# 384 dense columns, 40 tiles turned ahead, and loads and norm in other places: a hybrid attention, mLSTM and expert step

## What is computed

```
x = x + merge(attention(xn), mlstm(xn))           # xn = rmsnorm(x) * g1, one input projection
q = (xn @ wq).reshape(nb, 8, 2, 64)               # xn = rmsnorm(x) * g2
s = einsum('nhpd,hpkd->nhpk', q, sub_keys)        # 128 keys on each side
sv, si = top_k(s, 16)
cand = sv[:, :, 0, :, None] + sv[:, :, 1, None, :]
fv, fi = top_k(cand, 16)                          # 16 of 16384 experts for each of 8 heads
eidx = experts of fi;  g = softmax(fv)
act = gelu(einsum('nhkd,nd->nhk', peer_u[eidx], xn))
x = x + einsum('nhk,nhkd->nd', g * act, peer_v[eidx])
```

## Time and profile before

| | us |
|---|---|
| runs | 2080.23, 2080.6, 2068.4; median 2080.23 |
| profiled execution | 2077.23, span 2075.5, mean granted clock 0.961 |
| PE, PEld busy in the span | 1922.2 (93%), 1819.3 (88%) |
| DVE, ACT, POOL busy | 1344.6 (65%), 892.0 (43%), 963.4 (46%) |
| moved by DMA | 478.80 MB, mean 231 GB/s |

### The profile page before, as it was taken

The page is one execution under the profiler, slowest core; times in us unless marked ns, Lnnn a source line. Parts: engine busy times, 40 slices in busy tenths (PEclk is TensorE's granted clock), DMA queues, the critical chain, the costliest instruction groups (busy, mean ns, idle before and its releaser), DMA issues. The chain is left out here.

```text
span 2075.5 us, 32520 instructions
## 1 busy us (share of the span) xinstructions
PE 1922.2 (93%) x11569; PEld 1819.3 (88%) x11569; DVE 1344.6 (65%) x2582; ACT 892.0 (43%) x1936; POOL 963.4 (46%) x840
## 2 busy tenths in 40 slices
PE   7999959998896999999999999998799999999997
PEld 6978748886895999898998899997799999999996
DVE  2134435555513299798999766774387877777775
ACT  4031113234304245677777777774233333333333
POOL 4433303332221257789999999995022222222210
PEclk9999979998997999999999999999899999999999
DMA  7611187786407145698999899999599999999982
GB/s 170 123 52 47 36 221 232 234 242 220 149 21 152 35 148 181 215 283 264 276 290 281 257 285 297 291 301 289 186 318 355 328 348 338 346 346 331 356 300 82
DMA packets 325245, 478.80 MB, mean 231 GB/s; under 512 B 37436, under 2 KB 249916, under 8 KB 321756
## 3 DMA queue, kind: packets, MB, share of 16 engines
q1 hardware_dynamic: 288220, 342.49, 53.9%
q0 software_dynamic: 36864, 134.23, 20.2%
HBM read 391.52 MB, written 83.96 MB: 229 GB/s over the span
## 5 line engine op out<-in xcount | busy, mean ns | idle before, releaser
L1413 PE MATMUL ps<-x_high,uT_high 128*128 128x416 f32 x1024 | 373.8, 365 | 20.6 <-DVE uT_low L1400 17.9
L1670 POOL TENSOR_SCALAR area<-iota_row,chosen 128x128 f32<-128x128 f32 x416 | 387.1, 944 | 3.2
L2013 PE MATMUL ps<-hid_high,v_high 128*128 128x416 f32 x1024 | 360.1, 352 | 12.7 <-DVE hid_low L1986 12.7
L1413 PE MATMUL ps<-x_high,uT_low 128*128 128x416 f32 x1024 | 364.5, 356 | 0.0
L1413 PE MATMUL ps<-x_low,uT_high 128*128 128x416 f32 x1024 | 361.9, 353 | 0.0
L2013 PE MATMUL ps<-hid_low,v_high 128*128 128x416 f32 x1024 | 359.9, 351 | 0.0
L2013 PE MATMUL ps<-hid_high,v_low 128*128 128x416 f32 x1024 | 359.7, 351 | 0.0
L1281 POOL DMA_INDIRECT gathered_rows<-in_peer_v_dram,gathered_index x128 | 134.9, 1054 | 430.5 <-DVE gathered_acc L1318 350.4
L1957 ACT CAST v_high<-area 128x1024 fp32r<-128x1024 f32 x128 | 134.3, 1049 | 390.8 <-PE ps L2013 386.9
L1984 DVE TENSOR_TENSOR v_low<-area,v_high 128x1024 fp32r<-128x1024 f32 x128 | 156.8, 1225 | 138.0 <-ACT v_high L1957 138.0
L1296 DVE SCALAR_TENSOR_TENSOR gathered_rows<-gathered_rows,gathered_x 128x1024 f32<-128x1024 f32 x128 | 163.9, 1287 | 85.3 <-DMA gathered_rows<-in_peer_u_dram,gathered_index 83.9
(11 more groups left out here) (293 smaller groups left out, 3917.6 us busy)
## 6 DMA issues: line engine op xcount, KB each, us to landing
area<-in_peer_v_dram SPq DMA_DIRECT2D x128, 512.0 KB, 5.3
u_nat<-in_peer_u_dram SPq DMA_DIRECT2D x392, 128.0 KB, 5.8
hidden<-gelu_out SPq DMA_DIRECT2D x128, 208.0 KB
routing<-dense SPq DMA_DIRECT2D x26, 1024.0 KB, 7.0
area<-hidden SPq DMA_DIRECT2D x120, 208.0 KB, 7.2
w_raw<-in_w_in_dram SPq DMA_DIRECT2D x44, 512.0 KB, 5.4
mv_nat<-in_peer_u_dram SPq DMA_DIRECT2D x120, 128.0 KB, 3.3
u_nat<-turned_u SPq DMA_DIRECT2D x30, 512.0 KB, 3.9
```

Of the source, the lines that this page charges most:

```text
L1413: ins = self.nc.tensor.matmul(self.k.ps[:, b, 0:N], w[:, b, kk, :], x[:, kk, 0:N], start=(kk == 0 and p == 0), stop=(kk == KD - 1 and p == 2))
L1670: ins = nc.gpsimd.tensor_scalar(first[:, b % AREAS, f, :], iota[:, :], chosen[:, 0, c:c + 1], None, ALU.is_equal)
L2013: ins = nc.tensor.matmul(ps[:, kk, 0:N], v[:, b, kk * P:(kk + 1) * P], h[:, b, :], start=(n == 0 and p == 0), stop=(n == P - 1 and p == 2))
```

## The change

Numbers first: `AHEAD` 30 becomes 40, with `CLEAR` = 5 (the first of them is turned in unit 5 rather than 0, the last still in unit 39). `MORE` takes all 128 frames of one prompt tile instead of 32 + 64 of them, so N falls from 416 to 384, the routing from 104 to 96 batches (26 to 24 groups), and the fetches rise from 128 to 160 in each of `search` and `experts`; `COPIES` falls from 12 to 2. `ROUTED_BY` = 118 puts the end of the routing six steps earlier; with the 32 split frames gone, no batch runs before step 31 where eight had run in steps 19 to 26. The dots are still spread up to step 124, 1.6 a step instead of 1.28.

Order second: (1) in `project`, SP's queue around the start of attention; (2) the norm goes from `queries` to the end of `merge`, tile by tile behind the last column slices; (3) in `queries`, POOL casts the weights as well, two query products are put between PE's turns, and two PSUM banks instead of four take the results; (4) in `search`, the gelu slices for the experts are loaded one by one in steps 96 to 103, and the routing loads and the first v tiles stand at step 125.

```diff
-AHEAD = 30
+AHEAD = 40
 DOTS_FROM = 24
-MORE = [(P - 96, 32), (P - 64, 64)]
+CLEAR = 5
+MORE = [(0, P)]
 HALVED = min(lo for lo, _ in MORE)
 N = 3 * P + HALVED
...
-AHEAD_LOADS = 64 if HALVED else 48
+AHEAD_LOADS = 16 * (OCT + 2)
+ROUTED_BY = 118.0
...
-        return [n for n in range(AHEAD) if n * 2 * GATE_TILES // AHEAD == u]
+        return [n for n in range(AHEAD) if CLEAR + n * (2 * GATE_TILES - CLEAR) // AHEAD == u]
...
@@ merge, ACT and DVE @@
+            norm_scalar(nc, k, act, 1, squares, [out_added] * NT, [OUTS - NT + t + 1 for t in range(NT)])
...
+            statistics = norm_vector(nc, k, dve, 1)
             for u in range(OUTS):
...
+                if u >= OUTS - NT + 2:
+                    next(statistics)
+            for _ in statistics:
+                pass
@@ Plan @@
-                credit += min(2.0, max(0.9, rest / max(1.0, 124.0 - n)))
+                credit += min(2.0, max(0.9, rest / max(1.0, ROUTED_BY - n)))
...
-        self.ahead = max(n for n, l in self.routing.items() if BATCHES - LATE * GRP // FEW - 1 in l) + 5
+        self.ahead = max(self.final[-1] + 4, P - 4 * OCT)
+        self.last = max(max(self.routing) + 5, P - USLOTS)
@@ queries, POOL @@
+                raw = w[m // 4][:, :, (m % 4) * P:(m % 4 + 1) * P]
+                nc.gpsimd.tensor_copy(w_high[:, m % 2], raw).then_inc(w_high_done, 1)
...
@@ queries, PE @@
+            for u in range(FIRST_HALF):
+                turn(u)
+            query(0)
+            for u in range(FIRST_HALF, 2 * NT):
+                turn(u)
+            query(1)
...
@@ search, SP @@
-                if n == plan.ahead:
+                if n - plan.ahead in range(OCT):
...
+                    a = n - plan.ahead
+                    sp.dma_start(k.gelu_in[0][:, a, :], k.gelu_dram[a]).then_inc(k.in_loaded[0], 16)
+                if n == plan.last:
+                    sp.wait_ge(routed, BATCHES)
+                    for a in range(4):
+                        sp.dma_start(k.v_nat[:, a, :], peer_v[0, a * P:(a + 1) * P, :]).then_inc(k.v_loaded[a], 16)
+                        if a == 0:
...
+                            load_routing(sp, 0, NGRP // 2)
+                            load_routing(sp, NGRP // 2, NGRP)
```

More of the change, by code:

```diff
@@ L472, in _ @@
             sp.dma_start(n_sample[0, 0].rearrange("h d -> d h"), state[:, :, P]).then_inc(stored, 16)
[L473 to L476, removed]
+            for u in range(4, 2 * GATE_TILES):
                 for n in turned_at(u - 1):
@@ L1039, in merge @@
     OUTS = NT * D // W
+    squares = hold("squares", [P, NT, D])
     with nc.Block() as block:
@@ L1497, in _ @@
                 nc.scalar.copy(skT[:, 4 * g:4 * g + 4, :], ps[:, 6 + g, :].rearrange("p (h n) -> p h n", h=4)).then_inc(sk_out, 1)
[L1498 to L1505 removed]
+            for u in range(2, 2 * PH):
+                take_query(u)
             hidden.split_high(act, 0)
@@ L1509, in _, with turn @@
         def _(pe):
-            for u in range(2 * NT):
+            def turn(u):
                 t, g = divmod(u, 2)
@@ L1519, in _, with query @@
                 ins.then_inc(turned, 1)
+            def query(u):
+                m, h = divmod(u, 2)
+                pe.wait_ge(vec_out, 2 * NT if h else FIRST_HALF)
+                if u >= 2:
+                    pe.wait_ge(q_out, u - 1)
+                pe.wait_ge(w_low_done, m + 1)
+                for kk in range(KD):
+                    for p, (a, b) in enumerate(((w_high, k.x_high), (w_high, k.x_low), (w_low, k.x_high))):
+                        ins = nc.tensor.matmul(ps[:, 4 + u % 2, 0:HALF], a[:, m % 2, kk, :], b[:, kk, h * HALF:(h + 1) * HALF],
+                                               start=(kk == 0 and p == 0), stop=(kk == KD - 1 and p == 2))
+                ins.then_inc(q_done, 1)
+            for u in range(FIRST_HALF):
[4 more added lines that the diff above has]
+            query(1)
             pe.wait_ge(loaded, 16 * LOADS)
@@ L1524, in _, with scale @@
                 ins.then_inc(sk_done, 1)
-            pe.wait_ge(vec_out, 2 * NT)
-            for u in range(2 * PH):
-                m, h = divmod(u, 2)
-                if u >= 4:
-                    pe.wait_ge(q_out, u - 3)
-                pe.wait_ge(w_low_done, m + 1)
-                for kk in range(KD):
-                    for p, (a, b) in enumerate(((w_high, k.x_high), (w_high, k.x_low), (w_low, k.x_high))):
-                        ins = nc.tensor.matmul(ps[:, u % 4, 0:HALF], a[:, m % 2, kk, :], b[:, kk, h * HALF:(h + 1) * HALF],
-                                               start=(kk == 0 and p == 0), stop=(kk == KD - 1 and p == 2))
-                ins.then_inc(q_done, 1)
+            for u in range(2, 2 * PH):
+                query(u)
         @block.vector
         def _(dve):
-            for t in norm_vector(nc, k, dve, 1):
+            def scale(t):
                 r = ROWS[t]
@@ L1542, in _ @@
                                         k.rstd[0:r, t:t + 1], None, ALU.mult).then_inc(normed, 1)
+            for t in range(3):
+                scale(t)
             dve.wait_ge(loaded, 16 * LOADS)
```

71 lines of the change are left out of this document (33 added, 38 removed).

## The result

The changed kernel takes 2157.0 us (2149.2 to 2168.8), before 2078.0 beside it: a ratio of 1.040, interval 1.037 to 1.043. The forecast was 2097 with a range of 2040 to 2145: within the 1% that it took for no change, though slower had the largest single chance, 0.40. The profiled execution took 2149.2 us, its span is 2147.5, 72 us over the span of before.

| stage | before, us | after, us | moved | forecast |
|---|---|---|---|---|
| to the last product of attention | 496.8 | 511.0 | +14 | -11 |
| from there to the search's step 0 (merge, queries) | 215.8 | 216.8 | +1 | +4 |
| search, steps 0 to 30 | 164.0 | 152.4 | -12 | -12 |
| search, steps 31 to 117 | 518.4 | 586.0 | +68 | +72 |
| search, step 118 to its last product | 64.1 | 52.0 | -12 | -16 |

The account below looks back on a forecast made before the run. It took POOL, not only PE's columns, to be full in the search's middle. From 2077 us, -11 +4 -12 +72 -16 -4 -13 gave 2097 us, range 2040 to 2145.

Parts of the forecast that it names:

- Projection, forecast -11: Projection and attention: filling PE's hole at attention's start gives -15, late turns cost +4; in all -11 us (-15 to +5).
- 1.14 tiles a unit: Attention: turning 40 tiles in 35 units, 0.75 a unit before, adds some 80 GB/s, a DMA share of 1.08.
- the turns saturate the DMA: Rival, projection: it gives back nothing, +10 instead of -11, all else as summed, 2118 us; chance 0.13.
- Search, steps 0 to 30, and its end: Search: eight batches leave steps 0 to 30, -12 us; cheaper routing loads and spread gelu slices at its end, -16.
- Search, middle, +72: Search, steps 31 to 117: 28 more compares, 27 more gathers and their dots load POOL, +72 us (+35 to +105).
- The 0.60 us of excess per dot: Search middle: POOL's compare excess of 120 us over 200 DVE dots and subtracts; 27 added dots cost +16.
- Two signs named ahead: Search middle: POOL over 95% busy would show its term right; compares shorter beside fewer columns would make the forecast fall.
- waits of DVE for gathers above 100 us: Sign in the search's middle: it would make the second rival right, that three gather buffers bind in both stages.
- Experts, forecast -13: Experts: PE alone gives -43 us, but ring and bytes stand in the way; -13 taken (-43 to +15), near the ring's price.
- The ring's price: Experts: add, issue and landing make 9.5 us for three rows; at 1.4 rows a tile, 4.45 us a tile.
- the bytes' at 566 us: Experts: 197 MB to move takes 566 us at 348 GB/s, or 524 at the best 376 GB/s.
- the three gather buffers bind in both stages: Rival: gathers without lead hold DVE, the search's middle costs +105, the experts lose 10; 2153 us, chance 0.25.

Follow-up runs that it names:

- e6: Changed kernel with 34 instead of 40 tiles turned ahead, so no unit turns two: attention ends at 480 us, the whole takes 2127.0 us, ratio 1.025.
- e5: Kernel before with 40 instead of 30 tiles turned ahead, one a unit, nothing else: attention ends at 498 us, the whole takes 2073.8 us, ratio 0.999.
- e3: Kernel before with only the projection's part of the change, still 30 tiles: attention ends at 475 us, the whole takes 2062.1 us, ratio 0.992.
- e15: Kernel before plus the change's rearrangements in projection, merge, queries and search, with 416 columns, 34 tiles and routing to step 122: 2049.5 us, ratio 0.988.
- e4: Changed kernel with the frames of before (416 columns, 128 gathers a stage): search middle 529.7 us, experts 580.8 us, the whole 2089.9 us, ratio 1.005.
- e1: Changed kernel with four gather buffers instead of three: search middle 578 us, experts 570 us, the whole 2110.9 us, ratio 1.017.
- e8: Changed kernel with each dot of the search on 512 of the 1024 columns: the search's middle takes 536 us instead of 586.
- e13: Changed kernel, three buffers, loading only half of each v tile in the experts from tile 4 on: experts 567 us instead of 599.
- e9: Changed kernel with four gather buffers, loading only half of each v tile in the experts from tile 4 on: experts take 535 us.

## Why the forecast was wrong, step by step

The two steps named below, in the projection and in the experts, make 56 us; between the sum of 2097 and the profiled execution lie 52.

*Projection, forecast -11, measured +14.* The step that failed is "1.14 tiles a unit". The code has no such unit: it has 30 with one tile and five with two, and a double unit needs its second tile before the queue can have brought it. Without double units attention ends 31 us sooner (e6, 480 against 511). The order of SP and the formula of `turned_at` said so, without a trace. The two ends set for late turns, 0 and +15, were drawn for a loaded DMA; e5 shows 276 GB/s at a share of 0.91 without harm, so the rival "the turns saturate the DMA", with its +10, came near this stage's +14 for the wrong reason. The gain that the step did name is real and was too low: 21 us in e3.

*Merge and queries, +4 against +1*: right in size, and e15 shows that the edits neither help nor harm.

*Search, steps 0 to 30, and its end*: -12 and -16 against -12 and -12. The stall of the earlier trace rows went, as said.

*Search, middle, +72 against +68.* Right in size, right in part in its cause, and partly by luck. e4 puts 56 us on the frames, and e1, where PE waits 71 us for POOL and 7 for DVE, shows POOL's work holding the stretch at 578. But the changed kernel does not spend the 68 us as summed. POOL is busy 50 us more and idle 18 us more: its compares take 10.5 us more where 17 were summed, its gather issues 40 where 39 were summed, and the 16 us that the added dots should take from it do not show, since a compare's mean fell from 951 to 918 ns. Two signs named ahead spoke against the term: POOL is busy 89% of the stretch, not over 95%, and the compares became shorter beside fewer columns. PE's waits are shared by POOL and by DVE's late work.

The 0.60 us of excess per dot, my average over dots and subtracts, was too low as a price: by e8 a whole dot of 1.27 us costs POOL about 1.1, an estimate from 0.85 us for each us of dot. With 1.1 the sum would have been about +85, 17 over; where POOL got that back was not traced.

*A sign that misled.* I had written that waits of DVE for gathers above 100 us would show the buffers at fault. They were 127 us, and a fourth buffer did bring PE's wait for DVE from 42 to 7 us; but the middle fell by only 8, and in all such runs by 6 to 24 (578 and 580 with four buffers, 586 to 602 with three). DVE still waits 93 us for gathers in e1, and the reading that fits is that POOL, busy 538 of 578 us, issues them late. Here the long wait in an in-order queue named the next link, not the first.

*Experts, forecast -13, measured +18.* The ring's price was worked out at 4.45 us a tile with the landing time of the kernel before, and the bytes' at 566 us; I took the larger of two limits as if the other were hidden by it. Each comes out nearly as priced where the other is eased: e13, with a quarter of a megabyte less a tile, takes 567 / 128 = 4.43 us, and e1, with four buffers, takes 570 us. With both in place it is 599. The step that failed is the choice between them: a landing time is not a constant beside a bandwidth. From e13 to the changed kernel the core moves 325 GB/s instead of 287, a landing takes 6.78 us instead of 6.17, and each round of the ring is that much longer.

That e13 hits the ring's 4.45 is luck in part. The landing time of the earlier trace rows is counted from the start of the issue, so the sum of 9.5 us, which adds the issue's 1.05, has it twice; what it leaves out is in the table of rounds, part of the 1.2 us before the add and the 0.9 us from the add to the next issue. The slips cancel: e13's round is 9.54. In the rival "the three gather buffers bind in both stages" (2153) the experts' +10 was the right mechanism; its +105 in the middle was too much, and that its time agrees with the measured one is luck, by the projection's 25 us.

The 566 us for the bytes rest on the 348 GB/s of the earlier trace rows, moved over 100 us at a DMA share of 1.00. In e1 the core moved 369 GB/s for 300 us of the experts (1600 to 1900), at a share of 1.02, so 348 is not the most that it moves:

```profile
DMA packets 59398, 110.73 MB, mean 369 GB/s; under 512 B 4167, under 2 KB 38872, under 8 KB 59375
```

## What to carry to other kernels

Where work is spread by an integer formula, write out the list that it makes before taking the average: one slot with two items in a two-deep pipeline can cost more than the average load (here the unit near 346 us and its follower took 9.2 + 6.5 us, where two others take 10). When two limits of a loop share a resource (here a ring's round trip and the DMA that it runs on), don't take the larger: ask what the one does to the other's terms. Moving work off a busy engine needs the price on every engine that takes it: 32 columns less saved PE 0.36 us a tile of the experts (e9's 535 us against 581), and the gathers that they became cost the search's middle 56 us for 29 of them, some 2 us each.

## What the runs showed of the hardware

The issue of a gather on POOL is not of constant length. In the experts the rows read, before and in the changed kernel (ns: least, median, most):

```profile
L1281 POOL DMA_INDIRECT gathered_rows<-in_peer_v_dram,gathered_index x128: 935/939/1792, 1440.5 to 2004.8; - x128
```

```profile
L1298 POOL DMA_INDIRECT gathered_rows<-in_peer_v_dram,gathered_index x160: 937/1618/2117, 1503.6 to 2088.5; - x160
```

The same instruction, 0.68 us longer at the median, though DVE is hardly busier (77% of the stretch against 75%). What differs is what DVE is doing when the issue begins. Before, DVE mostly waits at that moment; in the changed kernel it is often within the subtract `v_low`, which has two operands in SBUF, the engines' on-chip memory (before first):

```profile
1701.88 0.94 POOL L1281 DMA_INDIRECT gathered_rows<-in_peer_v_dram,gathered_index  x1 [3.59 <-DVE gathered_acc L1318]
1702.71 1.23 DVE L1984 TENSOR_TENSOR v_low<-area,v_high 128x1024 fp32r<-128x1024 f32 x1 [1.13 <-ACT v_high L1957]
```

```profile
1702.18 1.22 DVE L2011 TENSOR_TENSOR v_low<-area,v_high 128x1024 fp32r<-128x1024 f32 x1
1702.60 1.62 POOL L1298 DMA_INDIRECT gathered_rows<-in_peer_v_dram,gathered_index  x1 [2.59 <-DVE gathered_acc L1335]
...
1709.51 0.94 POOL L1298 DMA_INDIRECT gathered_rows<-in_peer_v_dram,gathered_index  x1 [1.65 <-DVE gathered_acc L1335]
1709.59 1.23 DVE L2011 TENSOR_TENSOR v_low<-area,v_high 128x1024 fp32r<-128x1024 f32 x1 [0.41 <-ACT v_high L1984]
```

Counted over the experts, all 95 issues of before and all 42 of the changed kernel that begin while DVE is idle take 0.94 to 0.95 us; the 101 of the changed kernel that begin within `v_low` take 1.29 to 2.12, 1.62 at the median, and the 14 of before 1.33 to 1.67. In the changed kernel's search middle 24 begin within a transpose, which has one operand: 22 take 0.94 to 1.03, and two, which begin in its last 0.03 us, 2.04. No run changes this alone, and why the issue is longer beside `v_low` was not shown.

Behind one stall of PE its granted clock was lower: after the 2.43 us of idling in attention came 3.6 us of product matmuls at a clock of 0.50, one every 0.23 us instead of 0.125, and the unit and its follower took 9.2 + 6.5 instead of 10 us. The mean clock over the search's middle was 0.94 in the changed kernel, where PE idles 85 us, and 0.99 before, where it idles 26.
